# Start addresses of the dense operands in SBUF: layer 0 from residue 0 to 192, layer 1 from residue 64 to 128 (modulo 256 bytes)

## The chip, the core and the metric
The kernel runs on one core of one Trainium2 chip. The metric is the device time in microseconds (us) of one execution. TensorE is called PE here (its weight loads PEld), VectorE DVE, ScalarE ACT, GpSimd POOL, and SyncE SP.

## What is computed
The reference is a two-layer decoder trunk on 512 tokens of width 1024. Each layer has a token mixer and an MLP with a squared ReLU, each modulated by a conditioning vector; layer 0 mixes with a gated linear recurrence (HGRN2), layer 1 with forgetting attention (FoX), and a final norm ends it. Cut to what matters:

```
for i in range(2):
    sh1, sc1, g1, sh2, sc2, g2 = split(silu(c) @ w_mod[i] + b_mod[i], 6)
    h = rmsnorm(x, norm1_w[i]) * (1 + sc1) + sh1
    y = hgrn2_mixer(h, ...) if i == 0 else fox_mixer(h, ...)   # h @ w_in, mixing, @ w_out
    x = x + g1 * y
    h = rmsnorm(x, norm2_w[i]) * (1 + sc2) + sh2
    x = x + g2 * (relu(h @ mlp_w1[i]) ** 2 @ mlp_w2[i])
return rmsnorm(x, final_w)
```

Everything is float32.

## The kernel before
**Matmuls.** All activations are kept transposed in SBUF: the partition is a feature of a block of 128, the free dimension the 512 tokens. Each dense product is made of float32r matmuls with both operands split in a high and a low part: for each block of 128 features `product` (L756 to L763) runs three matmuls, high weights by high activations (L761), high weights by low activations (L762) and low weights by high activations (L763). The weights, 128 columns of `whi` or `wlo`, are the stationary operand, and 512 tokens of the activations are the moving one; in the turnovers between sub-layers only 256 tokens at a time (`half_block`, and the first part of `mlp`). Where a token-major result is wanted (`quarter_token`, L861 to L863, and `token_half`, L1165 to L1167) the roles are changed: 128 tokens of h0 or h2 are stationary and 256 columns of `whi` or `wlo` move. The forget gate (L1177 to L1179) has stationary weights of its own.

**Names.** Layer 0 has h0 (input of the mixer), y0 (its output), h1 (input of the MLP) and a0 (squared activations of half of the MLP); layer 1 has h2, y1, h3 and a1. Each is a pair, as h0hi and h0lo. hq, hk, hf, hv, hgate and adiag belong to the recurrence, whose small matmuls are plain float32 (L922 to L965), and qt, kt, qhi, khi, vt, prob, pT to the attention.

**Feeding.** SP streams 208 blocks of 512 KB of weights into the four buffers of `raw`. For each, ACT copies raw to whi (L356) and DVE subtracts to get wlo (L1291), one quad of four blocks ahead of PE. DVE also computes the modulation rows from `mring` (L1282). The order of the work on each engine is written out by hand, with semaphores between the engines. The first 45 us are a head in which x, the first rows of the modulation (`modf`) and the first weights arrive.

**Where tiles lie.** SBUF tensors are laid one behind the other in the order in which the code opens them, as in a stack; closing an ExitStack gives its space back. x begins at byte 16512 of each partition, and raw, whi and wlo follow, so each of them begins at a multiple of 256 bytes plus 128. This distance from a multiple of 256 is called the residue. After the common tiles (par to acc) the end is at 93760, residue 64. There layer 1's tiles begin (h2hi, h2lo, qt and the rest, and a1, h3 in the same space), and since each has a size that is a multiple of 256, all have residue 64. Layer 0's `mring`, `cb`, `masks`, `lbc` and `mtmp` begin at the same 93760 and take 14016 bytes; h0hi behind them begins at 107776, residue 0, and so do h0lo, modf, hq to adiag, y0, h1, a0, wf and wfs. Blocks of 128 or 512 tokens within a tile begin 512 or 2048 bytes apart, at the same residue.

Of the kernel before, what the change touches and what calls it, by code (L numbers as in the profile page):

```python
# [6 lines left out]
F32 = mybir.dt.float32  # L7
# [6 lines left out]
P = 128  # L14
# [33 lines left out]
def build(nc, x_t, stream, mod_rows, w_forget, params, out_t):  # L48
    keep = ExitStack()
    with keep:  # L50
# [3 lines left out]
        def sb(name, shape, dt, ctx=keep):  # L54
            return ctx.enter_context(nc.sbuf_tensor(name, shape, dt))
# [22 lines left out]
        sqb = sb("sqb", [P, T], F32)  # L78
        acc = sb("acc", [P, T], F32)

        layer0 = ExitStack()
        mring = sb("mring", [P, 2, D], F32, layer0)
        cb = sb("cb", [P, D], F32, layer0)
        masks = sb("masks", [P, MASKED, P], U8, layer0)
        lbc = sb("lbc", [P, 6 * KT], F32, layer0)
        mtmp = sb("mtmp", [P, P], F32, layer0)

        hg = ExitStack()
        h0 = [sb(n, [P, KT, T], F32R, hg) for n in ("h0hi", "h0lo")]
# [1696 lines left out]
```

## Time and profile before
| | us |
|---|---|
| median of 3 runs | 1428.87 |
| lowest to highest | 1428.70 to 1429.33 |
| the profiled execution | 1429.67 |
| its span, first to last instruction | 1427.9 |
| PE busy | 1393.0 (98%) |
| DVE busy | 760.6 (53%) |
| ACT busy | 501.0 (35%) |
| POOL busy | 159.1 (11%) |

The mean granted clock of TensorE is 0.988 of full speed, 2.4 GHz. The chain of work that ended last lies to 91% on PE, 5% on DVE and 2% on ACT. Matmuls overlap: the durations of one that a list gives are longer than the distance from one start to the next, so where the engine is never idle the spacing of the starts in the timeline is what counts. Matmul records can be missing in a trace in small numbers; the trains used here have none missing, as their lines L761, L762, L763 follow each other in turn.

### The profile page before, as it was taken

To read this page: it belongs to the slowest core of one execution; us is meant where nothing else is said; L and a number is where in the kernel's file an instruction comes from. 1 tells how busy PE (TensorE), PEld (TensorE's weight loads), DVE (VectorE), ACT (ScalarE), POOL (GpSimd) and SP (SyncE) were. 2 spreads that over 40 slices of the span, in tenths; PEclk is the share of its full clock that TensorE was granted. 3 is DMA by queue.
4 is the path that set the end of the run, shared out by engine and by line. 5 is a ranking of instruction groups with operands and counts; after the bars stand their busy time and mean duration, and the time that the engine had idled before them with its cause. 6 is when DMAs were issued, how large, how long until landed. Compare 5 with 4: busy or idle time off the path is not lost.

```text
span 1427.9 us, 21924 instructions
## 1 busy us (share of the span) xinstructions
PE 1393.0 (98%) x8184; PEld 1207.8 (85%) x8184; DVE 760.6 (53%) x1342; ACT 501.0 (35%) x772; POOL 159.1 (11%) x206
## 2 busy tenths in 40 slices
PE   6899999999999999999999999999999999999997
PEld 4779898989988888888899998998898888888887
DVE  7664757564776446663356555555556432344333
ACT  5613242413443212432236454544335321233220
POOL 7151505050000000000001101010000000000000
PEclk8999999999999999999999999999999999999998
DMA  9433333321265456553214122212123322323311
GB/s 378 162 126 119 134 122 129 119 75 59 96 244 181 150 201 220 189 191 102 89 60 149 60 90 73 91 60 70 46 78 103 98 93 88 103 88 91 99 60 59
DMA packets 47496, 169.44 MB, mean 119 GB/s; under 512 B 5168, under 2 KB 7344, under 8 KB 46912
## 3 DMA queue, kind: packets, MB, share of 16 engines
q1 hardware_dynamic: 46816, 164.21, 33.8%
q10 hardware_dynamic: 608, 4.23, 0.8%
q8 instruction: 50, 0.82, 0.2%
q14 instruction: 22, 0.18, 0.0%
HBM read 166.29 MB, written 2.13 MB: 118 GB/s over the span
## 4 chain that ended last, share of the span: by engine, by line
PE 91%; DVE 5%; ACT 2%; issue 1%; DMA 1%; POOL 0%; SPq 0%; POOLq 0%; DVEq 0%; ACTq 0%
PE bank L761 22%; PE bank L762 21%; PE bank L763 21%; PE bank L861 3%; PE bank L862 3%; PE bank L863 3%; PE bank L932 3%; PE bank L1142 2%; PE bank L1112 1%; PE bank L1128 1%; PE bank L951 1%; DVE modf L1344 1%; DVE wlo L1291 1%; DVE scr L1266 1%; PE bank L1165 1%
## 5 line engine op out<-in xcount | busy, mean ns | idle before, releaser
L356 ACT ACTIVATE whi<-raw 128x1024 fp32r<-128x1024 f32 x204 | 215.3, 1055 | 264.8 <-PE bank L763 254.6
L1291 DVE TENSOR_TENSOR wlo<-raw,whi 128x1024 fp32r<-128x1024 f32 x205 | 252.5, 1245 | 16.7 <-ACT whi L356 16.7
L699 POOL TENSOR_TENSOR rst<-ssq,mhalf 128x8 f32<-128x8 f32 (+2 forms) x29 | 42.3, 1468 | 1129.1 <-DVE ssq L1244 944.9
L1552 DVE TENSOR_TENSOR scr<-scr 128x512 f32<-128x512 f32 x64 | 44.3, 692 | 126.7 <-ACT scr L526 126.7
L761 PE MATMUL bank<-h3hi,whi 128*128 128x512 f32 (+1 forms) x288 | 107.6, 374 | 1.1 <-DVE h3lo L1271 1.0
L761 PE MATMUL bank<-h1hi,whi 128*128 128x512 f32 (+1 forms) x288 | 106.8, 371 | 0.9 <-DVE h1lo L1271 0.6
L762 PE MATMUL bank<-h3lo,whi 128*128 128x512 f32 (+1 forms) x288 | 107.2, 372 | 0.0
L763 PE MATMUL bank<-h3hi,wlo 128*128 128x512 f32 (+1 forms) x288 | 107.2, 372 | 0.0
L761 PE MATMUL bank<-a0hi,whi 128*128 128x512 f32 (+1 forms) x288 | 106.5, 370 | 0.0
L763 PE MATMUL bank<-a0hi,wlo 128*128 128x512 f32 (+1 forms) x288 | 106.5, 370 | 0.0
L762 PE MATMUL bank<-a0lo,whi 128*128 128x512 f32 (+1 forms) x288 | 106.5, 370 | 0.0
L761 PE MATMUL bank<-a1hi,whi 128*128 128x512 f32 (+1 forms) x288 | 106.5, 370 | 0.0
L762 PE MATMUL bank<-h1lo,whi 128*128 128x512 f32 (+1 forms) x288 | 106.4, 369 | 0.0
L763 PE MATMUL bank<-h1hi,wlo 128*128 128x512 f32 (+1 forms) x288 | 106.4, 369 | 0.0
L762 PE MATMUL bank<-a1lo,whi 128*128 128x512 f32 (+1 forms) x288 | 106.3, 369 | 0.0
L763 PE MATMUL bank<-a1hi,wlo 128*128 128x512 f32 (+1 forms) x288 | 106.3, 369 | 0.0
L526 ACT ACTIVATE scr<-bank 128x512 f32<-128x512 f32 x64 | 38.2, 597 | 192.4 <-PE bank L763 192.3
L1282 DVE CUSTOM_DVE_ANT_0 mring<-mring,cb 128x1024 f32<-128x1024 f32 x80 | 98.5, 1239 | 2.5 <-DMA mring<-mod_rows 2.5
L861 PE MATMUL bank<-whi,h2hi 128*128 128x256 f32 x320 | 93.5, 292 | 0.0
L761 PE MATMUL bank<-h0hi,whi 128*128 128x512 f32 x192 | 82.0, 427 | 11.1 <-DVE h0lo L1251 11.1
L1445 DVE SCALAR_TENSOR_TENSOR x<-bank,mod,x 128x256 f32<-128x256 f32 (+1 forms) x44 | 26.5, 603 | 119.8 <-PE bank L763 119.7
L862 PE MATMUL bank<-whi,h2lo 128*128 128x256 f32 x320 | 89.3, 279 | 0.0
(255 smaller groups left out, 3183.6 us busy)
## 6 DMA issues: line engine op xcount, KB each, us to landing
raw<-stream SPq DMA_DIRECT2D x208, 512.0 KB, 4.1
mring<-mod_rows SPq DMA_DIRECT2D x80, 512.0 KB, 3.6
modf<-mod_rows SPq DMA_DIRECT2D x16, 512.0 KB, 15.2
fb<-negf ACTq DMA_DIRECT2D x4, 1024.0 KB, 5.6
x<-x_t SPq DMA_DIRECT2D x4, 512.0 KB, 5.9
out_t<-x SPq DMA_DIRECT2D x8, 256.0 KB, 2.2
wf<-w_forget SPq DMA_DIRECT2D x1, 512.0 KB, 5.0
par<-params SPq DMA_DIRECT2D x1, 86.0 KB, 2.0
```

What stands on the lines that cost most here:

```text
L356: S.activation(whi[:, j, :], raw[:, j, :], ACT.Copy).then_inc(w_hi, 1)
L699: G.tensor_tensor(rst[:, at:at + n], ssq[:, at:at + n], mhalf[:, 0:n], ALU.pow).then_inc(done, 1)
L761: PE.matmul(out, wh, hh[0], start=first, stop=False)
L762: PE.matmul(out, wh, hh[1], start=False, stop=False)
L763: return PE.matmul(out, wl, hh[0], start=False, stop=last)
L861: PE.matmul(o, hh, whi[:, j, w0], start=k == 0 and t % 2 == 0, stop=False, skip_group_check=True)
L862: PE.matmul(o, hl, whi[:, j, w0], start=False, stop=False, skip_group_check=True)
L863: mm = PE.matmul(o, hh, wlo[:, j, w0], start=False, stop=k == KT - 1, skip_group_check=True)
L932: mm = PE.matmul(second_halves(cols(ps[j], t), m), cols(kk, t), second_halves(cols(qq, t), m), start=True, stop=True)
L1282: V.tensor_tensor_reduce(out=mring[:, s, :], in0=mring[:, s, :], in1=cb[:, :], scale=1.0, scalar=0.0, op0=ALU.mult, op1=ALU.add, accum_out ...
L1291: V.tensor_tensor(wlo[:, j, :], raw[:, j, :], whi[:, j, :].bitcast(F32), ALU.subtract).then_inc(w_lo, 1)
L1552: V.tensor_tensor(scr[j % 2][:, :], scr[j % 2][:, :], scr[j % 2][:, :], ALU.mult).then_inc(ff_sq, 1)
```

## The change
A tile of 64 bytes per partition that nothing uses is opened behind the common tiles, and another one of 128 bytes behind mtmp, in layer 0's part:

```
@@ -78,12 +78,15 @@
         sqb = sb("sqb", [P, T], F32)
         acc = sb("acc", [P, T], F32)
 
+        sb("spacer0", [P, 16], F32)
+
         layer0 = ExitStack()
         mring = sb("mring", [P, 2, D], F32, layer0)
         cb = sb("cb", [P, D], F32, layer0)
         masks = sb("masks", [P, MASKED, P], U8, layer0)
         lbc = sb("lbc", [P, 6 * KT], F32, layer0)
         mtmp = sb("mtmp", [P, P], F32, layer0)
+        sb("spacer1", [P, 32], F32, layer0)
 
         hg = ExitStack()
         h0 = [sb(n, [P, KT, T], F32R, hg) for n in ("h0hi", "h0lo")]
```

Layer 1's tiles, and mring, cb, masks, lbc and mtmp, now begin 64 bytes higher: h2hi at 93824, residue 128. h0hi and the rest of layer 0's operands begin 192 bytes higher: h0hi at 107968, residue 192. x, raw, whi, wlo and the common tiles stay where they were. [...] Each engine's list of instructions is the same as before, in the same order.

## Rows read from the trace of the kernel before
**Rows 1.** The page, busy us (share of the span) xinstructions: PE.
```profile
PE 1393.0 (98%) x8184; PEld 1207.8 (85%) x8184; DVE 760.6 (53%) x1342; ACT 501.0 (35%) x772; POOL 159.1 (11%) x206
```
**Rows 2.** Busy us by stage (window, length, PE, PEld, DVE, ACT, POOL, PEclk, DMA share, GB/s).
```profile
0.00:45.00 45.00, 28.98 (x116) 23.42 (x116) 33.74 (x62) 23.94 (x35) 33.70 (x58) 0.81 0.86 341
...
470.00:725.00 255.00, 255.00 (x1182) 210.59 (x1181) 126.54 (x178) 69.20 (x87) 0.70 (x1) 1.00 0.45 157
```
**Rows 3.** Groups by line and shape: out<-moving,stationary xcount | busy us, mean ns | idle before.
```profile
L761 PE MATMUL bank<-h3hi,whi 128*128 128x512 f32 x224 | 88.6, 396 | 0.0
...
L761 PE MATMUL bank<-h0hi,whi 128*128 128x512 f32 x192 | 82.0, 427 | 11.1 <-DVE h0lo L1251 11.1
...
L761 PE MATMUL bank<-h2hi,whi 128*128 128x512 f32 x64 | 27.1, 424 | 0.0
...
L761 PE MATMUL bank<-y0hi,whi 128*128 128x512 f32 x32 | 13.5, 421 | 0.0
...
L861 PE MATMUL bank<-whi,h2hi 128*128 128x256 f32 x320 | 93.5, 292 | 0.0
...
L861 PE MATMUL bank<-whi,h0hi 128*128 128x256 f32 x128 | 36.6, 286 | 0.5 <-DVE wlo L1291 0.5
...
L1165 PE MATMUL bank<-whi,h2hi 128*128 128x256 f32 x64 | 18.1, 283 | 0.0
...
L761 PE MATMUL bank<-y0hi,whi 128*128 128x256 f32 x64 | 18.3, 286 | 0.0
```
**Rows 4.** Timeline of PE, layer 0, 512 columns (start us, duration us, instruction).
```profile
599.86 0.39 PE L763 MATMUL bank<-h1hi,wlo 128*128 128x512 f32 x1
...
639.59 0.40 PE L763 MATMUL bank<-a0hi,wlo 128*128 128x512 f32 x1
639.83 0.40 PE L761 MATMUL bank<-a0hi,whi 128*128 128x512 f32 x1
```
**Rows 5.** Timeline of PE, layer 1, 512 columns.
```profile
1240.06 0.40 PE L763 MATMUL bank<-h3hi,wlo 128*128 128x512 f32 x1
...
1279.96 0.39 PE L763 MATMUL bank<-h3hi,wlo 128*128 128x512 f32 x1
```
**Rows 6.** Timeline of PE, 256 columns of y0 (layer 0) and y1 (layer 1).
```profile
344.14 0.28 PE L761 MATMUL bank<-y0hi,whi 128*128 128x256 f32 x1
...
352.54 0.28 PE L762 MATMUL bank<-y0lo,whi 128*128 128x256 f32 x1
...
1033.95 0.28 PE L761 MATMUL bank<-y1hi,whi 128*128 128x256 f32 x1
...
1039.95 0.28 PE L763 MATMUL bank<-y1hi,wlo 128*128 128x256 f32 x1
```
**Rows 7.** Timeline of PE, weights moving, h0 (layer 0) and h2 (layer 1) stationary.
```profile
61.83 0.28 PE L861 MATMUL bank<-whi,h0hi 128*128 128x256 f32 x1
...
67.17 0.28 PE L861 MATMUL bank<-whi,h0hi 128*128 128x256 f32 x1
...
758.53 0.28 PE L861 MATMUL bank<-whi,h2hi 128*128 128x256 f32 x1
...
763.83 0.28 PE L861 MATMUL bank<-whi,h2hi 128*128 128x256 f32 x1
...
901.78 0.28 PE L863 MATMUL bank<-wlo,h2hi 128*128 128x256 f32 x1
...
904.16 0.28 PE L863 MATMUL bank<-wlo,h2hi 128*128 128x256 f32 x1
```
**Rows 8.** Timeline of PE, float32 matmuls of hq and hk, two in a row.
```profile
113.28 0.59 PE L938 MATMUL bank<-hq,hk 128*128 128x256 f32 x2
...
114.58 0.59 PE L939 MATMUL bank<-hq,hk 128*128 128x256 f32 x2
```
**Rows 9.** Groups of DVE by line and shape, the low parts of h1 and h3.
```profile
L1271 DVE SCALAR_TENSOR_TENSOR h1lo<-scr,mod,h1hi 128x256 fp32r<-128x256 f32 x16 | 7.0, 482 | 1.8 <-ACT h1hi L362 1.8
...
L1271 DVE SCALAR_TENSOR_TENSOR h3lo<-scr,mod,h3hi 128x256 fp32r<-128x256 f32 x16 | 7.0, 483 | 1.8 <-ACT h3hi L362 1.8
```

More of the change, by code:

```diff
@@ L79, in build @@
         acc = sb("acc", [P, T], F32)
+        sb("spacer0", [P, 16], F32)
         layer0 = ExitStack()
@@ L86, in build @@
         mtmp = sb("mtmp", [P, P], F32, layer0)
+        sb("spacer1", [P, 32], F32, layer0)
         hg = ExitStack()
```

## Prediction
> **What bounds the kernel now.** I read the page's busy shares first. PE is busy in 98% of the span of 1427.9 us [rows 1]. The table by stage says the same of every stage but the head: between 470 and 725 us PE is busy 255.00 of 255.00 us, DVE 126.54 and ACT 69.20, and only the first 45 us, where the granted clock is 0.81 and the DMA share 0.86, have real holes (29.0 us busy) [rows 2]. Of the waits of PE in the dense groups the largest is 11.1 us, at h0 [rows 3]. So the time is the number of matmuls times the spacing from one start to the next. The durations in the grouped rows (395 ns for 512 columns) overlap and can't be summed, so I take spacings from the timeline instead: first and last start of an unbroken train, divided by the steps between them.
>
> Of 512 columns there are, in layer 0, h1, a0 (224 each a line), h0 (192) and y0 (32): 672 on each of the three lines, 2016 in all. In layer 1 they are h3, a1 (224 each), h2 (64) and y1 (32): 544 times three, 1632 [rows 3]. Of 256 columns, where the layer's operand is the moving one, layer 0 has y0, a0 and h1, 64 times three each (576), layer 1 has y1, a1 and h3 (576; the 48 of L1177 to L1179 are left out). Where it is the stationary one and the weights move, layer 0 has 384 and layer 1 has 960 plus 192, 1152 [rows 3]. Of groups with one count one row stands.
>
> The spacings, with the start residue modulo 256 of the operand in brackets:
> - 512 columns, layer 0 (0): 599.86 to 639.83 in 172 steps, 232.4 ns. Layer 1 (64): 1240.06 to 1279.96 in 171 steps, 233.3 ns [rows 4, 5].
> - 256 columns, layer 0 (0): 344.14 to 352.54 in 70 steps, 120.0 ns. Layer 1 (64): 1033.95 to 1039.95 in 53 steps, 113.2 ns [rows 6].
> - 256 columns with the weights moving, layer 0: 61.83 to 67.17 in 45 steps, 118.7 ns. Layer 1: 758.53 to 763.83 in 45 steps, 117.8 ns, and in another train of the very same operands, 901.78 to 904.16 in 21 steps, 113.3 ns [rows 7].
>
> The instructions of the two layers in the first two lines are the same in form; only the start of the operand differs. So the start is seen in the time: 1 ns in 232, and 7 ns in 120, with opposite signs. For comparison, the float32 matmuls of hq and hk with 256 columns, two instructions each, have six starts in 1.30 us, 217 ns apart [rows 8]. I take the 16 ns between 217 and 233 as an estimate of what in a dense spacing could depend on how the operands are read. This is the pot from which the change can give or take: 16 ns times 3648 is 58 us.
>
> **A page against the rows.** The rows show two spacings for one instruction at two addresses. The Trainium skill, TensorE: Matmul & The Clock Gate, section "Step-by-step: what each phase is for", says that the load of the next weights and the streamed operand have read ports of their own, so that the load takes nothing from the running matmul. By that rule no residue would matter and the time would stay at 1428.9; the 120.0 against 113.2 speak against it, and the sum below goes by the rows.
>
> **The change part by part.** It adds two unused tiles of 64 and 128 bytes. Every engine runs the same instructions in the same order with the same waits; only line numbers grow by three. No instruction is added, and the memory they take costs no time. What moves is where tiles begin. The weights whi and wlo stay at residue 128. Seen from the weights, layer 0's operands stood 128 ahead and will stand 64 ahead; layer 1's stood 192 ahead and will stand at the same residue, 0. Where the weights are the moving operand, the distance is counted the other way: layer 0 from 128 to 192, layer 1 from 64 to 0.
>
> DVE and ACT read and write the moved tiles, and I cost this at nothing: h1lo and h3lo take 482 and 483 ns at residues 0 and 64 [rows 9], and both engines have half their time free. The transfers into mring and modf begin elsewhere, too. The only place that they bound is the head; its PE wait is on DVE's h0lo, 11.1 us in all [rows 3]. I bound it by 1 us either way and take 0. The fp32 matmuls among the tiles of one layer keep their distances, as both operands move together.
>
> So everything is in the spacings. Of the four distances the rows show 128 (layer 0, both roles), 192 and 64 (layer 1). What I build on is that 64 and 192 look alike: both have trains at 113 ns and trains at 118, while distance 128 has 119 to 120 in either role. That is how it would be if the pattern repeated after 128 bytes. Then distance 0 acts as 128 did, and 64 as 192 did: the layers trade places.
> - Layer 0: 2016 times +0.95 ns is +1.9 us; 384 of y0 and a0 from 120.0 to 113.2, -2.6; the 192 of h1 and the 384 token matmuls from 118.7 to 117.8, -0.5. Sum -1.2.
> - Layer 1: 1632 times -0.95 is -1.6; 384 of y1 and a1 from 113.2 to 120.0, +2.6; 192 of h3 and 1152, 1344 in all, from 117.8 to 118.7, +1.2. Sum +2.2.
> Net +1.0 us: 1429.67 (the profiled execution, its span of 1427.9 and 1.8 around it) becomes 1430.7, and the median of the runs, 0.8 below it, becomes **1429.9**. Which of its two spacings each train falls into isn't fixed by the operands [rows 7], and this alone leaves 1427 to 1434 open in this case.
>
> **The rivals.**
> - *The new distances let the two reads pass each other: faster.* For it: 16 ns of each spacing are not needed by the columns, and one layer-1 train already shows that the same operands can run at 113.3 instead of 117.8 [rows 7]. Against it: the 512 columns, most of the time, differ by only 0.4% between two residues. With every 256-column train in the quick spacing: layer 0 +1.9 -2.6 and 576 times -5.4, -3.1; layer 1 -1.6 and 1344 times -4.5, -6.0. Sum -11.4, 1417.5; half of it, 1423, is what I take for the case.
> - *The stationary and the moving operand of layer 1 begin at one residue and get in each other's way from the first element: slower.* The place is every dense matmul after 725 us. The longest step that a 512-column train shows is 0.24 (639.59 to 639.83) [rows 4]; if all of layer 1 ran so, 6.7 times 1632 is +10.9, and its 256 columns at 120.0, 384 times 6.8 and 1344 times 2.2, +5.6. With layer 0's -1.2 that is +15.3, 1444; half of it, 1437, is what I take. It decides from 2.5 ns a matmul on: (2.9 + 1.2) us over 1632. Against it: at the two known distances a train of 170 steps averages 1 ns apart from the other, so steps of 0.24 are rare in both.
> - *The start has no part in it*, and the layers differ for another reason (other work beside them): the change does nothing for the time, 1428.9. Against it: the spacings repeat step by step over 40 us, whatever DVE, ACT and the DMAs do meanwhile.
>
> **How the numbers follow.** 0.2% of this kernel, 2.9 us, is about what a measurement can tell from no change. The traded places have a chance of 0.35 (0.29 within 0.2%, 0.05 slower, 0.01 faster), no effect 0.09, the faster rival 0.32 (0.02 of it within), the slower one 0.24 (0.02 within). Together faster 0.31, same 0.42, slower 0.27. Neither of the two new distances has a row with 512 columns at full height, so the range reaches well into both rivals: 1418 to 1438. The likeliest case by itself spans 1427 to 1434.
>
> **What would show it.** Right: in the trace of the changed kernel trains of h1 and a0 at 233.3 ns, of h3 and a1 at 232.4, of y0 and a0 with 256 columns near 113, of y1 and a1 near 120; PE's waits as now. The faster rival shows as spacings of 512 columns under 231 or token matmuls at 113 throughout. The slower one shows as layer 1 above 235. No effect shows as the same four numbers as now. The forecast would be wrong in kind if spacings stayed and the holes of PE changed, in the head above all.

## The result and the profile after

| | before | after |
|---|---|---|
| median of 6 runs, us | 1428.58 | 1416.20 |
| lowest to highest, us | 1427.90 to 1429.33 | 1414.33 to 1418.10 |
| the profiled execution, us | 1429.67 | 1417.89 |
| its span, us | 1427.9 | 1416.1 |
| granted clock over the span | 0.988 | 0.987 |

The ratio is 0.9914, with an interval from 0.9901 to 0.9927: the changed kernel is 12.4 us faster. The forecast was 1429.9 and a range from 1418 to 1438, so the time lies below both.

The first line of the page of the changed kernel, busy us (share of the span) xinstructions, answers [rows 1]:

```profile
PE 1381.0 (98%) x8184; PEld 1209.5 (85%) x8184; DVE 760.5 (54%) x1342; ACT 501.2 (35%) x772; POOL 159.1 (11%) x206
```

PE does the same 8184 matmuls in 12.0 us less busy time, and the span is 11.8 us shorter. DVE, ACT and POOL did not move by more than 0.2 us. The groups by line and shape (the columns of [rows 3] and [rows 9]; lines are three higher than before):

```profile
L764 PE MATMUL bank<-h3hi,whi 128*128 128x512 f32 x224 | 87.1, 389 | 0.0
L764 PE MATMUL bank<-h0hi,whi 128*128 128x512 f32 x192 | 81.9, 427 | 11.3 <-DVE h0lo L1254 11.3
L864 PE MATMUL bank<-whi,h2hi 128*128 128x256 f32 x320 | 94.4, 295 | 0.0
...
L1274 DVE SCALAR_TENSOR_TENSOR h3lo<-scr,mod,h3hi 128x256 fp32r<-128x256 f32 x16 | 7.0, 481 | 1.8 <-ACT h3hi L365 1.8
```

The wait of PE in the head is 11.3 us (before 11.1), and DVE's operation on h3lo takes 481 ns (before 483). No wait of PE changed by more than 0.4 us, and the side engines are as they were. What changed is inside the trains: h3 with 512 columns fell from 88.6 to 87.1 us a line, whi by h2 with 256 columns rose from 93.5 to 94.4.

The starts in the timeline of PE say by how much (start us, duration us, instruction). First the trains that answer [rows 4] and [rows 5]:

```profile
599.94 0.39 PE L764 MATMUL bank<-h1hi,whi 128*128 128x512 f32 x1
...
640.00 0.39 PE L765 MATMUL bank<-a0lo,whi 128*128 128x512 f32 x1
...
1240.03 0.39 PE L765 MATMUL bank<-h3lo,whi 128*128 128x512 f32 x1
...
1279.92 0.39 PE L764 MATMUL bank<-h3hi,whi 128*128 128x512 f32 x1
```

175 steps in 40.06 us are 228.9 ns (before 232.4), and 176 steps in 39.89 us are 226.6 ns (before 233.3). Then those that answer [rows 6] and [rows 7], again of PE's timeline after:

```profile
341.43 0.28 PE L765 MATMUL bank<-y0lo,whi 128*128 128x256 f32 x1
...
349.47 0.28 PE L764 MATMUL bank<-y0hi,whi 128*128 128x256 f32 x1
...
1025.95 0.28 PE L766 MATMUL bank<-y1hi,wlo 128*128 128x256 f32 x1
...
1035.91 0.28 PE L765 MATMUL bank<-y1lo,whi 128*128 128x256 f32 x1
...
56.25 0.28 PE L865 MATMUL bank<-whi,h0lo 128*128 128x256 f32 x1
...
66.46 0.28 PE L865 MATMUL bank<-whi,h0lo 128*128 128x256 f32 x1
...
748.83 0.28 PE L1168 MATMUL bank<-whi,h2hi 128*128 128x256 f32 x1
...
756.99 0.28 PE L866 MATMUL bank<-wlo,h2hi 128*128 128x256 f32 x1
```

y0 runs at 113.2 ns (71 steps; before 120.0), y1 at 120.0 (83 steps; before 113.2), the token matmuls of h0 at 113.4 (90 steps; before 118.7) and those of h2 at 120.0 (68 steps; before 117.8 or 113.3).

One train is not a mean, so here are the mean spacings of each family over all its unbroken steps, in ns. "Distance" is, here and below, the start of the layer's operand minus that of the weights, modulo 256 bytes.

| kernel | distance, layer 0 / 1 | h1, a0 512 | h3, a1 512 | h0 512 | h2, y1 512 | y0, a0, h1 256 | y1, a1, h3 256 | tokens h0 | tokens h2 |
|---|---|---|---|---|---|---|---|---|---|
| before | 128 / 192 | 232.4 | 233.3 | 232.0 | 233.2 | 119.2 | 114.7 | 118.6 | 117.3 |
| after | 64 / 0 | 228.9 | 226.7 | 229.6 | 229.9 | 116.7 | 119.9 | 115.1 | 119.5 |

These are the means of one profiled execution. Times the counts of the prediction, they give most of the 12 us. With 512 columns, h1 and a0 give 1344 times -3.5, -4.7 us; h0 576 times -2.4, -1.4; h3 and a1 1344 times -6.6, -8.9; h2 and y1 288 times -3.3, -1.0. That is -16.0, without the 96 of y0. With 256 columns, layer 0 gives 576 times -2.5 and 384 times -3.5, -2.8, and layer 1 costs 576 times 5.2 and 1152 times 2.2, +5.5. The sum is -13.3, and the span moved by -11.8. Summed in the traces of before and after from each start to the next one, the broken steps (those next to a wait or another group) included, h0's 512 columns gave 0.4 us and not 1.4, y0's 96 matmuls of 512 columns took 0.9 us more, and h3's 256 columns cost nothing instead of 1.0, as their broken steps got shorter. The loss at y0 lies in a stretch where the granted clock fell (windows 300 to 320 us: length, then busy us of PE, PEld, DVE, ACT and POOL, the granted clock, DMA share, GB/s; the kernel before has a clock of 1.00 in both):

```profile
300.00:310.00 10.00, 8.68 (x49) 7.00 (x47) 7.67 (x14) 0.00 (x0) 6.94 (x11) 0.89 0.35 107
310.00:320.00 10.00, 9.66 (x55) 7.83 (x55) 2.71 (x6) 1.64 (x4) 3.53 (x6) 0.94 0.00 0
```

A second profiled execution of the same changed kernel (after_again) does not show that stretch: its span was 1412.1, its h0 gave 3.1 us and its y0 0.2. These two groups make 3.8 of the 4.0 us between the executions. The windows of both (the same columns), the first execution and the other:

```profile
0.00:45.00 45.00, 28.89 (x116) 23.35 (x116) 33.46 (x62) 24.02 (x35) 33.53 (x58) 0.81 0.87 341
45.00:330.00 285.00, 278.15 (x1756) 246.22 (x1757) 171.53 (x287) 87.19 (x125) 92.34 (x124) 0.98 0.34 117
```

```profile
0.00:45.00 45.00, 31.75 (x116) 25.79 (x116) 32.79 (x62) 23.73 (x35) 33.38 (x58) 0.96 0.87 341
45.00:330.00 285.00, 278.37 (x1784) 247.01 (x1785) 173.86 (x291) 88.61 (x127) 92.37 (x124) 1.00 0.34 117
```

The granted clock was 0.81 in the head and 0.98 up to 330 us in the first, 0.96 and 1.00 in the second, which has 28 more matmuls behind it at 330 us. So one profiled execution of this kernel stands for its time only to some 4 us. For the spacings of h1, a0, h3 and a1 with 512 columns it stands to a tenth of a nanosecond. For those of 256 columns it doesn't: the train of h0's token matmuls shown above, at 113.4 ns, ran at 117.8 in the second execution (85 steps), with the same instructions at the same addresses:

```profile
56.44 0.28 PE L865 MATMUL bank<-whi,h0lo 128*128 128x256 f32 x1
...
66.45 0.28 PE L866 MATMUL bank<-wlo,h0hi 128*128 128x256 f32 x1
```

### The profile page after: what moved, and what is told of

It is laid out like the page before. It is cut to its first block, busy times and chain, and to the rows that moved or that the text cites. A ratio compares the mean times of both kernels' runs of the same rounds, so it can differ in the third digit from the quotient of the medians.

```text
span 1416.1 us, 21924 instructions
## 1 busy us (share of the span) xinstructions
PE 1381.0 (98%) x8184; PEld 1209.5 (85%) x8184; DVE 760.5 (54%) x1342; ACT 501.2 (35%) x772; POOL 159.1 (11%) x206
## 4 chain that ended last, share of the span: by engine, by line
PE 91%; DVE 4%; ACT 2%; issue 1%; DMA 1%; SPq 0%; POOL 0%; POOLq 0%; DVEq 0%; ACTq 0%
PE bank L764 22%; PE bank L765 22%; PE bank L766 21%; PE bank L864 3%; PE bank L866 3%; PE bank L865 3%; PE bank L935 3%; PE bank L1145 2%; PE bank L1115 1%; PE bank L1131 1%; PE bank L954 1%; DMA raw<-stream 1%; DVE modf L1347 1%; DVE wlo L1294 1%; PE bank L1168 1%
## 5 line engine op out<-in xcount | busy, mean ns | idle before, releaser
L1555 DVE TENSOR_TENSOR scr<-scr 128x512 f32<-128x512 f32 x64 | 44.3, 692 | 119.9 <-ACT scr L529 119.9
L864 PE MATMUL bank<-whi,h2hi 128*128 128x256 f32 x320 | 94.4, 295 | 0.0
L764 PE MATMUL bank<-h0hi,whi 128*128 128x512 f32 x192 | 81.9, 427 | 11.3 <-DVE h0lo L1254 11.3
L866 PE MATMUL bank<-wlo,h2hi 128*128 128x256 f32 x320 | 90.4, 282 | 0.0
```

What stands on the lines that cost most here:

```text
L764: PE.matmul(out, wh, hh[0], start=first, stop=False)
L864: PE.matmul(o, hh, whi[:, j, w0], start=k == 0 and t % 2 == 0, stop=False, skip_group_check=True)
L866: mm = PE.matmul(o, hh, wlo[:, j, w0], start=False, stop=k == KT - 1, skip_group_check=True)
L1555: V.tensor_tensor(scr[j % 2][:, :], scr[j % 2][:, :], scr[j % 2][:, :], ALU.mult).then_inc(ff_sq, 1)
```

## The experiments

Two questions: is the distance of the two operands the cause, and if so, what does each distance cost?

**Bare trains at sixteen distances (m1_trains).** The decoder is left out. One pair of weights stays where it is, and pairs of operands are placed every 32 bytes:

```
DISTANCES = range(0, 512, 32)
for d in DISTANCES:
    if d:
        sb(f"spacer{d}", [P, 8], F32)
    m[d] = [sb(f"d{d}{n}", [P, 2, T], F32R) for n in ("hi", "lo")]
...
for d in DISTANCES:
    moving(d, 512)        # 48 matmuls: whi*hi, whi*lo, wlo*hi, ...
    moving(d, 256)
    stationary(d, 256)    # the weights move
```

> This kernel leaves the whole decoder out: it has only trains of 48 float32r matmuls, in the order of product (high weights by high, high by low, low by high), with nothing else running, and copies x to the output. The operand begins 0, 32, 64 and so on up to 480 bytes ahead of the weights (modulo 512): for each distance one train of 512 moving columns, one of 256, and one of 256 with the weights moving. Theory (the spacing is made by the distance of the two operands alone): without other engines 512 columns give 226.7 ns at 0, 228.9 at 64 or 320, 232.4 at 128 and 233.3 at 192 or 448; 256 columns 120 at 0, 113 or 118 at 64, 120 at 128, 113 or 118 at 192. Rival (traffic of other engines makes the difference): one spacing, near 217, at every distance. What distances between the multiples of 64 do is open; if whole blocks of 64 bytes are what counts, 32 acts as 0 or as 64.

Mean spacing over the last 36 steps of each train, ns:

| distance | 0 | 32 | 64 | 96 | 128 | 160 | 192 | 224 |
|---|---|---|---|---|---|---|---|---|
| 512 columns | 226.7 | 233.3 | 228.9 | 233.3 | 232.3 | 234.4 | 233.3 | 233.3 |
| 256 columns | 120.0 | 116.7 | 117.8 | 120.0 | 118.7 | 117.4 | 113.3 | 118.5 |
| 256, weights moving | 120.0 | 118.3 | 117.8 | 120.0 | 118.6 | 120.0 | 117.8 | 116.7 |

Distances 256 to 480 repeat the first eight. In its timeline of PE, five trains of 512 columns:

```profile
30.62 0.39 PE L81 MATMUL bank<-d0lo,whi 128*128 128x512 f32 x1
...
39.01 0.39 PE L82 MATMUL bank<-d0hi,wlo 128*128 128x512 f32 x1
...
76.84 0.39 PE L81 MATMUL bank<-d64lo,whi 128*128 128x512 f32 x1
...
85.30 0.39 PE L82 MATMUL bank<-d64hi,wlo 128*128 128x512 f32 x1
...
123.67 0.39 PE L80 MATMUL bank<-d128hi,whi 128*128 128x512 f32 x1
...
131.81 0.39 PE L82 MATMUL bank<-d128hi,wlo 128*128 128x512 f32 x1
...
169.96 0.39 PE L82 MATMUL bank<-d192hi,wlo 128*128 128x512 f32 x1
...
178.36 0.39 PE L82 MATMUL bank<-d192hi,wlo 128*128 128x512 f32 x1
...
215.81 0.39 PE L81 MATMUL bank<-d256lo,whi 128*128 128x512 f32 x1
...
224.20 0.39 PE L82 MATMUL bank<-d256hi,wlo 128*128 128x512 f32 x1
```

The first and the last have 37 steps in 8.39 us, 226.8 ns each; distance 64 has 37 in 8.46, 128 has 35 in 8.14 (232.6), 192 has 36 in 8.40 (233.3). These are the four numbers of the kernel before and after. Its page shows that no other engine can have made them:

```profile
PE 372.6 (93%) x2400; PEld 338.1 (85%) x2400; DVE 10.3 (3%) x17; ACT 17.5 (4%) x18; POOL 0.2 (0%) x4
```

So with 512 columns the distance sets the spacing, to some 1 ns in the bare trains and in the long trains of h1, a0, h3 and a1, and the pattern repeats after 256 bytes, not 128: 0 and 128 are 5.6 ns apart. The likeliest case of the prediction falls here, and so does the slower rival: with 512 columns, operands at the same residue do not get in each other's way but run best. Distance 32 acts neither as 0 nor as 64, so whole blocks of 64 bytes are not what counts. With 256 columns the distance doesn't fix the spacing alone: at 192 it is 113.3 here and in m4_bytes, and 117.8 in m3_load_width, for the same form of matmul.

**Each layer alone (e1_layer1_only, e2_layer0_only).** e1 moves layer 1's operands only (mring, cb, masks, lbc and mtmp move with them):

```
         acc = sb("acc", [P, T], F32)
+        sb("spacer0", [P, 16], F32)
...
         mtmp = sb("mtmp", [P, P], F32, layer0)
+        sb("spacer1", [P, 112], F32, layer0)
```

> Layer 1's operands at residue 128 (distance 0 from the weights) as in the changed kernel, layer 0's at residue 0 (distance 128) as before. Theory: h3 and a1 at 226.7 ns, h1 and a0 at 232.4; about -10.2 us from the 512 columns of layer 1 and +5 from its 256 columns: 1424, 1422 to 1426. Rival (what helped is something in layer 0 or in the head, such as the start of the modulation rows): 1428.6.

e2 moves layer 0 only:

```
         mtmp = sb("mtmp", [P, P], F32, layer0)
+        sb("spacer1", [P, 48], F32, layer0)
```

> Layer 0's operands at residue 192 (distance 64) as in the changed kernel, layer 1's at 64 (distance 192) as before. Theory: h1 and a0 at 228.9 ns, h3 and a1 at 233.3; -7.0 us from the 512 columns of layer 0 and -2 from its 256 columns: 1420, 1418 to 1422; the two parts add up to the whole change. Rival (the parts don't add up, as the state at the end of layer 0 carries over): further than 2 us from that.

e1 took 1422.5 us, ratio 0.9955 (0.9938 to 0.9971), e2 1422.2, ratio 0.9947 (0.9930 to 0.9964). Against the 1428.9 of before, measured beside them, that is -6.4 and -6.7, together -13.1, and the whole change gives -12.4: the two parts add up within the intervals (some 2.4 us each way). Timeline of PE, e1, the changed layer:

```profile
1199.73 0.39 PE L764 MATMUL bank<-a1lo,whi 128*128 128x512 f32 x1
...
1234.87 0.39 PE L763 MATMUL bank<-a1hi,whi 128*128 128x512 f32 x1
```

155 steps at 226.7 ns; its h1 and a0, which did not move, kept 232.4. In e2 it is the other way, 228.9 in layer 0 and 233.3 in layer 1. By the spacings in the table above, layer 1 gives 9.9 us with 512 columns and its 256-column trains take 5.5 back, -4.4; layer 0 gives 6.1 and another 2.8, -8.9. The measured -6.4 and -6.7 are each some 2 us off, at the edge of what the intervals allow, and only the sum is well confirmed. Part of the difference lies in what the averages leave out: summed from start to start, layer 1's groups give 5.7 us in the trace of e1, as h3's 256 columns cost nothing, and layer 0's give 7.1 in that of e2, where y0's 96 matmuls again take 1.1 us more, at clocks of 0.89 and 0.94.

**The weights moved instead (e3_weights_moved).** All the experiments so far move the operands. A rival was that the operand's own residue counts. Here the operands keep the residues 0 and 64 of the kernel before, and raw, whi and wlo go to residue 0, which makes the distances 0 and 64 (the common tiles par to acc move by 128 bytes with them):

```
         x = sb("x", [P, KT, T], F32)
+        sb("spacer0", [P, 32], F32)
         raw = sb("raw", [P, 4, D], F32)
...
         acc = sb("acc", [P, T], F32)
+        sb("spacer1", [P, 96], F32)
```

> The operands of both layers keep their residues of before (0 and 64), and raw, whi and wlo go from residue 128 to 0. Theory (the distance counts): layer 0 is now at distance 0, 226.7 ns, layer 1 at 64, 228.9 ns; -11.5 and -7.2 us from 512 columns, 256 columns of layer 0 as before, of layer 1 as before or a little quicker: 1410, 1407 to 1413, which would be below the changed kernel. Rival (the residue of the activations by itself counts): spacings of 232.4 and 233.3 as before and 1428.6.

1412.1 us, ratio 0.9885 (0.9868 to 0.9901). Timeline of PE, e3, layer 0 and layer 1:

```profile
499.78 0.39 PE L763 MATMUL bank<-a0hi,whi 128*128 128x512 f32 x1
...
539.90 0.39 PE L763 MATMUL bank<-a0hi,whi 128*128 128x512 f32 x1
...
1269.64 0.39 PE L763 MATMUL bank<-h3hi,whi 128*128 128x512 f32 x1
...
1306.96 0.39 PE L764 MATMUL bank<-h3lo,whi 128*128 128x512 f32 x1
```

177 steps at 226.7 ns in layer 0 and 163 at 229.0 in layer 1: the operands lie as they did at 232.4 and 233.3, and of the tiles that these matmuls read only the weights moved. For 512 columns it is the distance. This kernel is also faster than the changed one.

**Three bare tests of how it comes about.** The first looks for a combination of the four tiles (whi fixed; wlo, hi and lo at each of four residues, 64 in all) that beats 226.7:

```
for a in RES:
    for b in RES:
        for c in RES:
            moving(wlo[a], hi[b], lo[c], 512)
            moving(wlo[a], hi[b], lo[c], 256)
            stationary(wlo[a], hi[b], lo[c], 256)
```

> Leaves the whole decoder out: trains of 48 matmuls alone, as before, now for all 64 combinations in which the low weights, the high and the low activations begin 0, 64, 128 or 192 bytes ahead of the high weights (modulo 256). Theory (each weight load meets the moving read that runs beside it, so every pair of neighbours has its own distance): spacings differ within one combination by the pair, and the 226.7 ns of distance 0 is not the least; some combination is below 225 ns. Rival (226.7 is the floor of this form of matmul): no combination below 226.5. For 256 columns: theory 113.3 is the floor already, since it is the load's own time.

None does. 512 columns run from 226.67 to 235.56, the next best being 228.86; 256 columns and weights moving from 113.33 to 121.5 and 121.1. My theory, a combination below 225, fell. Only one of the 64 combinations has 226.67, that with all four tiles at one residue: with lo alone 64 bytes further it is 232.1, and with wlo, hi and lo together at 192 it is 231.1, though the high weights are the only tile then at another residue. So the places of all four tiles count, and not the distance of one pair.

Many of the averages are whole or third parts of a step of 6.67 ns: 113.33 and 226.67 are 17 and 34 of them, 120.0 and 233.33 are 18 and 35, 228.89 and 117.78 lie one and two thirds above the lower ones. That is arithmetic on averages, and others don't fit it (232.25, 234.39 and 118.69 in m1_trains). The single steps don't show it either: the trace keeps starts to 1 ns, and at distance 64 the steps of 512 columns run from 225 to 232 ns, at 128 from 228 to 241.

The second takes away part of the load, by 128, 96, 64 or 32 stationary columns:

```
-                    w = slice(P * k, P * k + P)
-                    out = ps[i // 8][:, 0:n]
+                    w = slice(P * k, P * k + cols)
+                    out = ps[i // 8][0:cols, 0:n]
```

> Leaves the whole decoder out: trains of 48 matmuls with 128, 96, 64 or 32 stationary columns at distances 0, 64, 128 and 192, with 512 and with 256 moving columns. Theory (the load of the next weights and the running moving read hold each other up): with half the columns to load, the spacing of 512 columns falls by half of what it has over 216 ns, so to about 221 at distance 0 and 224 at 192, and at 32 columns to within 3 ns of 216, with differences between distances under 2 ns. Rival (the cost is the moving read's own): 226.7, 228.9, 232.3 and 233.3 at every width.

Spacing with 512 moving columns, ns:

| stationary columns | 0 | 64 | 128 | 192 |
|---|---|---|---|---|
| 128 | 227.4 | 228.9 | 233.3 | 233.3 |
| 96 | 230.0 | 233.3 | 226.7 | 228.3 |
| 64 | 230.0 | 228.3 | 231.1 | 232.8 |
| 32 | 231.7 | 231.7 | 230.5 | 231.7 |

I had expected that the cost falls with the size of the load. It doesn't: a quarter of the load costs 230.5 to 231.7. What moves is the best distance: with 96 columns, whose load ends 128 bytes earlier, it is 128 and not 0. Two trains of this kernel, timeline of PE, 96 stationary columns at distances 0 and 128:

```profile
87.94 0.39 PE L82 MATMUL bank<-d0hi,wlo 128*96 128x512 f32 x1
...
96.22 0.40 PE L82 MATMUL bank<-d0hi,wlo 128*96 128x512 f32 x1
...
122.08 0.39 PE L82 MATMUL bank<-d128hi,wlo 128*96 128x512 f32 x1
...
130.24 0.40 PE L82 MATMUL bank<-d128hi,wlo 128*96 128x512 f32 x1
```

36 steps each, 230.0 and 226.7 ns. That looks as if the end of the load counted and not its start, but 64 and 32 columns don't continue the pattern, so it stays a guess. The load itself did get shorter in the trace, from 0.19 us with 128 columns to 0.11 with 32.

The third changes the type (granted clock 1.0 throughout). The same trains once in float32r and once in bfloat16, with 512, 384, 256 and 128 columns:

```
+    b[d] = [sb(f"d{d}{n}", [P, 2, T], BF16) for n in ("bhi", "blo")]
...
+    moving(b[d], (bhi, blo), n)
```

> Leaves the whole decoder out: trains of 48 matmuls with 512, 384, 256 and 128 moving columns at distances 0, 64, 128 and 192, first in float32r and then in bfloat16, where both operands have half the bytes. Theory (two reads of four bytes an element get in each other's way): in bfloat16 512 columns take 216 ns at every distance, and the distance stops mattering; in float32r what is above columns over 2.4 grows with the columns (13 to 20 ns at 512, two thirds of it at 384). Rival (the cost lies in starting each matmul, whatever it reads): the same 11 to 20 ns in bfloat16 too, and the same at 384 and 512 columns.

| columns | float32r, distance 0 / 64 / 128 / 192 | bfloat16, every distance | columns by 2.4 GHz |
|---|---|---|---|
| 512 | 226.8 / 228.9 / 232.4 / 233.3 | 215.8 | 213.3 |
| 384 | 173.3 / 173.3 / 175.9 / 173.3 | 162.5 | 160.0 |
| 256 | 120.0 / 117.8 / 120.0 / 113.3 | 109.2 | 106.7 |
| 128 | 111.7 at every distance | 55.8 | 53.3 |

Timeline of PE, bfloat16 at distances 0 and 192, 45 steps of 215.8 ns each:

```profile
147.20 0.38 PE L89 MATMUL bank<-d0blo,bhi 128*128 128x512 bf16 x1
...
156.91 0.38 PE L89 MATMUL bank<-d0blo,bhi 128*128 128x512 bf16 x1
...
179.16 0.38 PE L90 MATMUL bank<-d192bhi,blo 128*128 128x512 bf16 x1
...
188.87 0.38 PE L90 MATMUL bank<-d192bhi,blo 128*128 128x512 bf16 x1
```

In bfloat16 the distance has no effect, and a matmul takes 2.5 ns over its columns, against 13.3 to 20 in float32r with 512 columns. The other half of my expectation failed: what is above the columns' time doesn't shrink by a third at 384 columns, it is 13.3 there at three of the four distances, and at 128 columns it is 58 ns. Nor does this test show that the bytes are the reason. The type changes more than the bytes: the recorded weight load takes 98 ns in bfloat16 and 188 to 197 in float32r, and whether the float32r matmuls with 128 columns, at 111.7, wait for their loads was not tested. The Trainium skill, TensorE: Matmul & The Clock Gate, "Back-to-back issue gap", gives the same N/2.4 plus 2.5 ns for an isolated matmul; the bfloat16 trains agree with it at all four sizes, each matmul with its own weight load, and the float32r trains agree at none. For a stream of loads and matmuls the same section of the Trainium skill gives some 81 ns with 128 columns and 131 with 512; these bfloat16 trains are such streams and ran at 55.8 and 215.8, and the measurement decides.

**Other distances in the kernel (after_again, e3_again, e5_both_0, e6_both_64).** By m1_trains distance 0 is best for 512 columns, 64 in second place, while for 256 columns 64 is better than 0. The changed kernel and e3 ran again beside two kernels with one distance for both layers. e5, distance 0:

```
         acc = sb("acc", [P, T], F32)
+        sb("spacer0", [P, 16], F32)
...
         mtmp = sb("mtmp", [P, P], F32, layer0)
+        sb("spacer1", [P, 16], F32, layer0)
```

e6, distance 64, has `[P, 32]` in place of the first `[P, 16]`.

> The changed kernel once more, beside the three below on one chip: 1416.2, 1414 to 1418.

> The kernel with the weights moved (layer 0 at distance 0, layer 1 at distance 64) once more. Theory: 4 us below the changed kernel, as in its first runs: 1412, 1409 to 1413. Rival (the first runs were a lucky chip): the same as the changed kernel.

> Weights at residue 128 and both layers' operands at 128 too, distance 0 throughout. If layers can be priced one by one: layer 0 -11.5 us from 2016 matmuls of 512 columns and +0.7 from 256 columns, layer 1 -6.4 as where it was moved alone: 1411.4, within 2 us of the kernel with the weights moved. If distance 0 is bad for 256 columns beyond that: above 1415.

> Both layers' operands 64 bytes ahead of the weights (residue 192). Layer 0 as in the changed kernel (-6.7 us where it was moved alone), layer 1 as with the weights moved (that kernel's -16.8 less layer 0's -10.8, so -6.0): 1416, the same as the changed kernel. The rival of a price that depends on what the other layer does would put it more than 2 us off.

| kernel | distance, layer 0 / 1 | us | ratio (interval) | h1, a0 512 | h3, a1 512 | 256, layer 0 / 1 | tokens h0 / h2 |
|---|---|---|---|---|---|---|---|
| after_again | 64 / 0 | 1415.6 | 0.9914 (0.9898 to 0.9931) | 228.9 | 226.7 | 116.7 / 119.9 | 116.2 / 119.5 |
| e3_again | 0 / 64 | 1412.6 | 0.9886 (0.9869 to 0.9902) | 226.7 | 228.9 | 119.9 / 116.9 | 119.9 / 115.4 |
| e5_both_0 | 0 / 0 | 1414.5 | 0.9905 (0.9888 to 0.9921) | 226.7 | 226.7 | 119.9 / 119.9 | 119.9 / 119.5 |
| e6_both_64 | 64 / 64 | 1414.4 | 0.9906 (0.9889 to 0.9922) | 228.9 | 228.9 | 116.0 / 117.8 | 115.1 / 114.9 |

The spacings of 512 columns are those of the bare trains in each of the four. The time of e5 was missed by 3 us: I expected 1411.4 and got 1414.5. I had priced all 2016 matmuls of 512 columns in layer 0 at 226.7 ns. Only h1 and a0 have that; h0's ran at 229.0 in unbroken steps, and h0 and y0 together gave 2.4 us in the trace where I had counted 3.8. By the spacings e5 against after gives -3.0 in h1 and a0 and takes back 576 times 3.2 and 384 times 4.8 ns, +3.7, in layer 0's 256 columns; so it should have been no better than after. e6, expected at 1416, came at 1414.4, inside the 2 us that I allowed. By the spacings it gives 1152 times -4.6 ns, -5.3, in the tokens of h2 and 576 times -2.1, -1.2, in layer 1's other 256 columns, against +3.0 in h3 and a1. That is -3.5 where the medians show -1.2. I had priced its layer 1 by subtracting one median from another, with no account of the 256-column trains. These fall into one of several spacings, and not always into that of the bare train. The kernel of e3 shows it too: the long train of a1's 256 columns ran at 117.8 ns in its first profiled execution and at 113.3 in e3_again, which is the same kernel.

**A distance for each family (e7_mixed).** The tiles that move 512 columns for most of their matmuls (h1, a0, h3, a1) get distance 0, and those that stand still in the token matmuls (h0, h2) get 64, with all that lies in the same part of the memory, y0 and y1 among it:

```
         acc = sb("acc", [P, T], F32)
+        sb("spacer0", [P, 16], F32)
...
         mtmp = sb("mtmp", [P, P], F32, layer0)
+        sb("spacer1", [P, 16], F32, layer0)

         hg = ExitStack()
+        sb("spacer2", [P, 16], F32, hg)
...
         fox = ExitStack()
+        sb("spacer3", [P, 16], F32, fox)
```

> Weights at residue 128. The operands that are read nearly always in 512 columns (h1, a0, h3, a1) at distance 0, those of the token-major products and the outputs of the mixers (h0, y0, h2, y1, and with them hq to adiag and qt to fb) at distance 64. If each group has the spacing of its own distance: h1, a0, h3 and a1 at 226.7 ns (6 us less than with both layers at 64), the token matmuls at 115 to 118, y0 and y1 at 115 to 118; 1408, 1406 to 1411, below all the others. Rival (the groups' trains are too mixed for their own spacing): 1412 to 1415.

1408.5 us (1407.7 to 1409.5), ratio 0.9858 (0.9841 to 0.9874). Its page's first line and two trains of PE's timeline, tokens of h2 at distance 64 and a1 at distance 0:

```profile
PE 1372.2 (98%) x8184; PEld 1204.1 (86%) x8184; DVE 761.1 (54%) x1342; ACT 500.9 (36%) x772; POOL 158.1 (11%) x206
```

```profile
742.97 0.28 PE L1170 MATMUL bank<-whi,h2lo 128*128 128x256 f32 x1
...
753.69 0.28 PE L867 MATMUL bank<-wlo,h2hi 128*128 128x256 f32 x1
...
1179.75 0.39 PE L765 MATMUL bank<-a1hi,whi 128*128 128x512 f32 x1
...
1218.96 0.39 PE L767 MATMUL bank<-a1hi,wlo 128*128 128x512 f32 x1
```

91 steps at 117.8 ns and 173 at 226.6. Over the kernel h1, a0, h3 and a1 run at 226.7 and the tokens at 115.1 and 115.2. Against after that is 1344 times -2.2 and 1152 times -4.3, -7.9, less 0.9 that a0's and h1's 256 columns take back and with 0.4 more from y1's. The measured difference is -7.1 against after_again and -7.7 against the first runs, and the time is the one expected. It beats both kernels, 20 us under before, with four unused tiles of 64 bytes.

## Why the prediction was wrong

- **What bounds the kernel: right.** PE's spacing times the number of matmuls gave the whole result. All twelve microseconds are PE's (1393.0 to 1381.0), and the other engines have the same times.
- **Nothing else moves: right.** DVE's operations, costed at nothing, take 481 and 482 ns; the wait at h0 is 11.3 us against 11.1, within the 1 us that bounded it.
- **The distance from the weights is what counts: right for 512 columns**, and shown by e3, where of the two operands only the weights moved. It was assumed in the prediction and could not be told there from the operand's own residue.
- **"The pattern repeated after 128 bytes": the step that failed.** It was read off the 256-column trains and applied to the 512 columns, for which no row existed at the new distances. Even for the 256 columns the rows said less: they have distance 192 only at 113.2, and 64 only with the weights moving. For the 256 columns it came out about right all the same: y0 went from 120.0 to 113.2 and y1 from 113.2 to 120.0 in the trains shown, h2's tokens from 117.3 to 119.5 on average. a0, forecast at 113.2 too, went to 117.8, and h0's tokens, forecast at 117.8, to 115.1. For the 512 columns the pattern repeats after 256, and 0 and 64 are the two good distances, 128 and 192 the two bad ones. The term of layer 0, 2016 times +0.95 ns or +1.9 us, measured -6.1 on the 1920 that were averaged; that of layer 1, 1632 times -0.95 or -1.6, measured -9.9. These are products of mean spacings and counts; with the broken steps of h0 and y0 in it, layer 0's 2016 gave 4.2.
- **The 1 ns between the layers was taken as the size of the effect.** Both known distances were on the bad side of the pattern, so their difference said nothing of how much there was to gain. The estimate of the pot, 16 ns a matmul, was sound as a bound: 6.6 of the 16 were given back in layer 1 and 3.5 in layer 0. No distance tried gave more; the shortest float32r spacing of any run here is 226.7 with 512 columns, 13.3 over the columns' own time.
- **The faster rival: right that the new distances are faster, right in its time by luck, wrong in its place.** Its 1417.5 is 1.3 off. But it put the gain into the 256-column trains, which together cost 2.7, and gave the 512 columns +0.3. The "512 columns under 231" that was named as its sign is what the trace shows.
- **The slower rival: wrong.** At one residue (distance 0) a 512-column train has its shortest spacing, 226.7. In the 256-column trains it does get in the way a little, 120.0 against 113.3 to 117.8, and this is its +5.6, which came out as +5.5 by the spacings and +4.5 summed in the trace.
- **The start has no part in it: wrong,** by every run above. The rule weighed beside it, that the load takes nothing from the running matmul, is that of the Trainium skill, TensorE: Matmul & The Clock Gate, "Step-by-step: what each phase is for". In bfloat16 the rows agree (215.8 at all distances). In float32r the spacing does depend on the distance from the weights (226.7 to 234.4), which the prediction had taken the rule to exclude; that it is the load that takes the time is not shown, as a quarter of the load costs no less.
- **The chances.** Of all the terms, the 3648 matmuls of 512 columns had the least evidence at the new distances, and they are most of the time. The likeliest case and its neighbours were built on the 2688 smaller ones.

Open stays why the spacing depends on the distance at all, why 96 stationary columns move the best distance by 128 bytes, why the short runs of h2 and y1 keep 229.9 at distance 0 where h3 and a1 have 226.7, and what puts a 256-column train into one of its spacings. The rule for 512 columns with 128 stationary ones is measured; its cause is not.

## What to carry to other kernels

In this kernel, which is bound by float32r matmuls, the start of the moving operand relative to that of the stationary one, modulo 256 bytes, is worth about 3% of the time of each dense train of 512 columns; unused tiles of 64 bytes set it, and a bare train of 48 matmuls for each distance prices it to some 1 ns, for the long trains. For 256 columns a bare train gives only one of the spacings that occur, so measure those in the kernel. Take the best distance for each shape apart (of the four tried in this kernel, 0 for 512 columns, 64 for 256 with the weights moving) and weigh by counts. Keep the high and low parts of an operand at one residue. When two values of a knob give nearly the same time, this doesn't say that the knob does little: look for the values that nobody has measured before a symmetry is assumed.

## What the runs showed of the hardware

- Float32r matmuls with a new load each take 226.7 to 234.4 ns with 512 columns by the distance of the two starts, 113.3 to 120.0 with 256 (m1_trains), and 111.7 with 128 at each of the four distances tried (m4_bytes). In m1_trains the pattern repeats after 256 bytes, and the odd multiples of 32 bytes are all bad for 512 columns (233.3 to 234.4).
- Bfloat16 matmuls show none of this: 215.8, 162.5, 109.2 and 55.8 ns with 512, 384, 256 and 128 columns.
- The best distance for 512 columns is no good one for 256 (120.0), and the best for 256 in m1_trains is no good one for 512 (192: 113.3 and 233.3).
- The same train of 256 columns at the same addresses can run at 113.4 ns in one execution and at 117.8 in the next (h0's tokens, after and after_again).
- With wlo, hi and lo placed apart from whi and from each other, 512 columns take up to 235.6 ns (m2_residues).
